# Reloading the attention heads' q, k and v inside the eighth RWKV iteration, with the cosine product on GpSimd

## What is computed

```
def _rope(x, pos):
    ...
    cos, sin = jnp.cos(ang)[:, None, :], jnp.sin(ang)[:, None, :]
    x1, x2 = x32[..., :half], x32[..., half:]
    return jnp.concatenate([x1 * cos - x2 * sin, x2 * cos + x1 * sin], axis=-1)
...
q_h = _rope(q_b.reshape(bsz, t_len, N_HEADS_B, HEAD_B), pos)
k_hb = _rope(k_b.reshape(bsz, t_len, N_HEADS_B, HEAD_B), pos)
v_hb = v_b.reshape(bsz, t_len, N_HEADS_B, HEAD_B)
```

## Time and profile before

| | |
|---|---|
| median of 3 runs | 2375.22 us (2374.91 to 2377.22) |
| the profiled execution | 2377.97 us, of which 2376.1 us is the span from the first to the last instruction |
| TensorE busy | 2279.6 us, 96% of the span |
| VectorE, ScalarE, GpSimd busy | 1151.1, 958.5 and 105.8 us |
| mean granted TensorE clock | 0.978 of full speed |
| eighth RWKV iteration | about 981 to 1058 us |
| head stage | about 1058 to 1087 us |
| cached pages, eight sequences | about 1087 to 1270 us |

### The profile page before, as it was taken

How to read it: one execution, slowest core, us unless ns; L and a number is a source line. 1 busy time by engine, 2 the same in 40 slices (tenths; PEclk the granted TensorE clock), 3 DMA queues, 4 the chain that set the end, 5 groups by cost and what they waited for, 6 DMA issues and landing times. The chain is left out here.

```text
span 2376.1 us, 49467 instructions
## 1 busy us (share of the span) xinstructions
PE 2279.6 (96%) x19735; PEld 2015.9 (85%) x19735; DVE 1151.1 (48%) x1907; ACT 958.5 (40%) x1413; POOL 105.8 (4%) x224
## 2 busy tenths in 40 slices
PE   6999899999999999978998999799999999999998
PEld 3889788887878878645666999799999999999998
DVE  4456635345353543425454655645545545544443
ACT  2433424334343443316553333454555554433333
POOL 0000001000000000100000000000100100000000
PEclk9999999999999999959998999999999999999999
DMA  9985556565666656567996555355555555555544
GB/s 347 308 286 148 160 182 182 178 192 178 191 184 187 187 171 198 185 206 245 381 388 235 165 164 160 106 163 164 168 163 164 168 163 164 168 164 164 161 151 127
DMA packets 328136, 461.20 MB, mean 194 GB/s; under 512 B 37432, under 2 KB 221282, under 8 KB 327538
## 3 DMA queue, kind: packets, MB, share of 16 engines
q1 hardware_dynamic: 319757, 450.22, 59.6%
q10 hardware_dynamic: 8215, 8.59, 1.1%
HBM read 442.86 MB, written 15.86 MB: 193 GB/s over the span
## 5 line engine op out<-in xcount | busy, mean ns | idle before, releaser
L954 ACT ACTIVATE whi<-raw 128x1024 fp32r<-128x1024 f32 (+1 forms) x512 | 527.2, 1030 | 893.1 <-PE ps L2021 861.8
L2021 PE MATMUL ps<-hhi,whi 128*128 128x288 f32 x2736 | 832.2, 304 | 10.0 <-DVE hlo L1479 6.4
L2021 PE MATMUL ps<-hhi,wlo 128*128 128x288 f32 x2736 | 808.0, 295 | 0.0
L2021 PE MATMUL ps<-hlo,whi 128*128 128x288 f32 x2736 | 807.3, 295 | 0.0
L1428 DVE TENSOR_TENSOR wlo<-raw,whi 128x1024 fp32r<-128x1024 f32 (+1 forms) x400 | 470.9, 1178 | 625.7 <-ACT whi L954 625.6
L2021 PEld LDWEIGHTS ps<-hhi,whi 128*128 128x128 f32 x2736 | 514.9, 188 | 73.0 <-issue 52.5
L2021 PEld LDWEIGHTS ps<-hlo,whi 128*128 128x128 f32 x2736 | 515.3, 188 | 1.2
L2021 PEld LDWEIGHTS ps<-hhi,wlo 128*128 128x128 f32 x2736 | 514.9, 188 | 0.0
L2021 PE MATMUL ps<-fhi,whi 128*128 128x288 f32 x704 | 208.2, 296 | 2.8 <-DVE wlo L1428 2.8
L2021 PE MATMUL ps<-fhi,wlo 128*128 128x288 f32 x704 | 207.7, 295 | 0.0
L2021 PE MATMUL ps<-flo,whi 128*128 128x288 f32 x704 | 207.3, 294 | 0.0
(11 more groups left out here) (399 smaller groups left out, 2753.6 us busy)
## 6 DMA issues: line engine op xcount, KB each, us to landing
raw<-in_w_up SPq DMA_DIRECT2D x352, 256.0 KB, 2.9
raw<-in_w_ada SPq DMA_DIRECT2D x128, 512.0 KB, 4.8
raw<-in_w_in SPq DMA_DIRECT2D x112, 512.0 KB, 4.5
raw<-in_w_down SPq DMA_DIRECT2D x88, 512.0 KB, 3.8
kpage<-in_cache_v SPq DMA_DIRECT2D x64, 512.0 KB, 5.9
raw<-in_w_in SPq DMA_DIRECT2D x72, 384.0 KB, 5.4
kpage<-in_cache_k SPq DMA_DIRECT2D x40, 512.0 KB, 5.2
ada_d<-in_w_ada SPq DMA_DIRECT2D x32, 512.0 KB, 5.9
```

The costliest lines, as they stand in the source:

```text
L954: return act.activation(o, i, ACT.Copy, **k)
L2021: return pe.matmul(out, lhsT, rhs, start=start, stop=stop, **k)
```

## The change

- The buffer `qk` gets the shape `[P, HB, 2, T]` (q and k of a head side by side) and another place: directly behind `osb`, so that its heads 0 to 3 don't overlap what the end of the eighth iteration still uses. `vq` keeps its place at the start of the region.
- v of all heads (one transfer, 1152 KB) is issued by SP within the eighth iteration, after slab 5 and the state stores there, once `mixed` and `spilled` allow it.
- q and k of heads 0 to 3 (two transfers of 576 KB) are issued when `send_turned` and `y_done` of the eighth iteration have come, ahead of the last `pair_stores`. q and k of heads 4 to 7 are issued after `ya_lo`, as before.
- TensorE's `rotate(0)` waits for `gn_roots`, the state rows and the load of heads 0 to 3. The waits for `ya_lo`, `ada_in_mod` and v come behind it.
- The product with cos moves from VectorE to GpSimd, one 128x576 operation for each head, which waits for `rotated` of that head; VectorE waits for it (`cos_done`) between its two remaining operations.
- The waits for the stores of the states move from SP to ScalarE, ahead of its first copy of k and v.

The places and the counts:

```
+        qk = nxt("qk", [P, HB, 2, T])
...
-        qk = nxt("qk", [P, 2 * HB, T])
...
-        HEADS_0 = ADA_X + 48
+        HEADS_0 = ADA_X + 32
...
+        COS_0 = KA * (LEVELS - 1)
+        HEAD0 = 64 * KA
+        EARLY_H = 4
```

SP's queue:

```
                 if s == 5:
                     pair_stores(j - 1)
+                    sp.wait_ge(mixed, KA)
+                    sp.wait_ge(spilled, 16 * RG * (KA - 1))
+                    sp.dma_start(vq[:, :, :], spill[2 * HB:3 * HB, :, :].rearrange("h p t -> p h t")).then_inc(lora_in, 16)
...
+
+            def heads_load(h0, h1, done):
+                for i in range(2):
+                    sp.dma_start(qk[:, h0:h1, i, :], spill[i * HB + h0:i * HB + h1, :, :].rearrange("h p t -> p h t")).then_inc(done, 16)
+
+            sp.wait_ge(send_turned, 2 * KA)
+            sp.wait_ge(y_done, KA)
+            heads_load(0, EARLY_H, heads_in[0])
             pair_stores(KA - 1)
-
-            def heads_load(h0, h1, done):
-                for dst, t in ((qk, 0), (qk, HB)):
-                    sp.dma_start(dst[:, t + h0:t + h1, :], spill[t + h0:t + h1, :, :].rearrange("h p t -> p h t")).then_inc(done, 16)
-                sp.dma_start(vq[:, h0:h1, :], spill[2 * HB + h0:2 * HB + h1, :, :].rearrange("h p t -> p h t")).then_inc(done, 16)
-
             sp.wait_ge(ya_lo, KA)
-            sp.wait_ge(sstate_out, 16 * NB * KA)
-            sp.wait_ge(pstate_out, 16 * KA)
-            sp.wait_ge(reloaded, ADA_X + 64)
-            heads_load(0, 1, reloaded)
-            heads_load(1, 3, heads_in[0])
-            heads_load(3, HB, heads_in[1])
-
+            heads_load(EARLY_H, HB, heads_in[1])
```

GpSimd, behind its eight iterations:

```
+            for h in range(HB):
+                pool.wait_ge(rotated, h + 1)
+                pool.tensor_tensor(qk[:, h, :, :], qk[:, h, :, :], c("cos").unsqueeze(1).to_broadcast([P, 2, T]), ALU.mult).then_inc(cos_done, 1)
```

ScalarE, ahead of its loop over the heads:

```
             act.wait_ge(reloaded, ADA_X + 64)
+            act.wait_ge(sstate_out, 16 * NB * KA)
+            act.wait_ge(pstate_out, 16 * KA)
```

VectorE, `rope`:

```
-                two = qk[:, h:2 * HB:HB, :]
+                two = qk[:, h, :, :]
                 b2 = 2 * (h % 2)
                 own.inc(TTn(rt, ps[:, b2:b2 + 2, 0:T], bc(c("sin").unsqueeze(1), [P, 2, T]), ALU.mult))
-                own(TTn(two, two, bc(c("cos").unsqueeze(1), [P, 2, T]), ALU.mult))
+                dve.wait_ge(cos_done, COS_0 + h + 1)
+                own.wait()
                 TTn(two, two, rt, ALU.add).then_inc(roped, 1)
```

TensorE, behind its eight iterations:

```
-            pe.wait_ge(ya_lo, KA)
+            pe.wait_ge(gn_roots, KA)
             pe.wait_ge(sstate_rows, 2 * KA)
             pe.wait_ge(pstate_rows, KA)
-            pe.wait_ge(ada_in_mod, ADA_G)
...
-                loaded = {0: (reloaded, ADA_X + 112), 1: (heads_in[0], HEADS_0), 3: (heads_in[1], HEADS_0)}
+                loaded = {0: (heads_in[0], HEADS_0), EARLY_H: (heads_in[1], HEADS_0)}
...
             rotate(0)
+            pe.wait_ge(lora_in, HEAD0 + 16)
+            pe.wait_ge(ya_lo, KA)
+            pe.wait_ge(ada_in_mod, ADA_G)
             for h in range(HB):
```

More of the change, by code:

```diff
@@ L526, in build @@
         tile_added = roped
+        cos_done = et_done
         stages = {}
```

12 lines of the change are left out of this document (6 added, 6 removed).

## The result

The changed kernel took 2371.51 us in the median of 11 runs (2367.45 to 2374.5), the kernel before, run beside it, 2377.28 in the median of 11 (2374.29 to 2382.4). The ratio is 0.9975 [0.9967, 0.9983]: 5.8 us less, where 7.8 had been forecast. The forecast time, 2367.4, was 4.1 us too low, and the range up to 2371.0 missed the median by 0.5 us. Part of that is not the change: the three runs of the kernel before from which I started had a median of 2375.22, and all 105 runs of it in this study have 2377.2. The profiled execution of the changed kernel took 2369.53 us, with a span of 2367.6.

What follows compares the result with a forecast made beforehand. The bound was taken to be the chain from group norm through `ya_lo`, head loads and eight heads to the first key page, with later stages following its start. 7.5 + 0.5 - 0.2 = 7.8 us less gave 2367.4 us, range 2364.5 to 2371.0.

Steps and rivals of the forecast that it cites:

- Rival D: Key pages: their transfers set the end whatever the start, so the change gives nothing, 2375 us; chance 2%.
- Part 1: Start of the head stage: early q and k loads make `rotate(0)` free and bring the first transpose 7.5 us earlier.
- just in time: State stores behind the early loads: landed by 1060.4 at the pessimistic end, ScalarE's first copy due about 1061; cost 0, at most 1 us.
- Part 2: Eighth iteration: the early v load fits an idle DMA gap and costs 0.2 us, between 0 and 3.3.
- Rival C: Eighth iteration: the v load falls into the full DMA stretch and 3.3 us go, 2370.5 us; chance 6%.
- Part 3: Head loop: the cosine on GpSimd, 1.21 us an operation, gains 0.5 us, between 0 and 1.6.
- rival B: Head loop: VectorE's two-input sums slow GpSimd's operation to 2.4 us; gain only 6.1 us, 2369.1 us; chance 6%.
- F: Head loop: GpSimd's operation becomes the cadence; slower from 3.3 us an operation, 2381 us at 4 us; chance 2%.
- A: Head stage: TensorE's lower clock stays for four more heads, 5.8 us go back, 2373.2 us; chance 7%.
- E: Head loop: ScalarE becomes the bound at 2.0 us a head, keys 9.5 to 10.1 us earlier, 2365.1 to 2365.7 us; chance 5%.
- the clock decides, not VectorE: Head loop: cadence 2.49 us with the lower clock until about 1065, 2.27 with the full clock throughout.

Runs made afterwards that it cites:

- the kernel held to `ya_lo`: Changed kernel with one wait more: GpSimd's first cosine product waits for `ya_lo`; 2370.99 us, ratio 0.9969 to the kernel before.
- loads alone: Changed kernel with the cosine product put back on VectorE, early loads kept; 2372.69 us, ratio 0.9969 to the kernel before.
- cosine alone: Kernel before with only the cosine product moved to GpSimd, loads as they were; 2375.74 us, ratio 0.9993.
- free-running ring: Changed kernel with `rotate(1)` also early and GpSimd's products written to four buffers of their own, not waiting for `rotated`; 2368.96 us, ratio 0.9971.
- side products: Early loads with the cosine on VectorE, plus three two-input GpSimd products beside the group norm; one trace, reciprocal to `yalo` 6.16 us against 4.41.

## Why the prediction was right and wrong

**What bounds the kernel: right.** The stage of the pages moved as a whole. Keys to the last values took 187.93 us before and 188.06 after, while it began 7.43 us earlier by the clock of the trace; over all sixteen traces that stage lies between 186.0 and 190.0 us, with the early loads or without. Rival D, that the transfers set the end whatever the start, is out.

**Part 1, 7.5 us: right in size, but not all of it is the loads'.** `yalo` to the first transpose fell from 10.20 to 2.76, 7.44 us (7.1 against the other trace of before, whose load came sooner). From the start of the reciprocal the forecast had the first transpose at 7.14 us (1059.83 less 1052.69); it was at 8.08, and at 7.17 in the kernel held to `ya_lo`, without the loss in the norm. The loads let `rotate(0)` begin at 1052.60, 5.8 us from their issue, 0.7 more than the 5.1 of my estimate. By the clock of the trace that was 1.4 to 2.4 us before the estimated time only because the issue came at 1046.81 and not at 1049.30. The store of the states, due "just in time", cost nothing: ScalarE's first copy, at 1062.12, waited for the transposes. But parts 1 and 3 are not two separate terms. Part 1 counted only the sine product and the sum for head 0, as if the cosine had moved already; with the cosine on VectorE "turn" falls by 6.93 and not by 7.44, and "heads" grows by 0.31 even with the clock back early (17.84 to 18.15). The sum of both parts was foreseen, 8.0, and the split of it was not: about 6.6 us for the loads, and 1.2 for GpSimd on top of them, of which the norm takes 0.9 back. The one trace of the loads alone as it stands says 5.6 for the loads, because the lower clock lasted longer in it.

**Part 2, 0.2 us: nothing that can be seen.** In three traces TensorE stood idle for the sixth pair of slabs, and it could start 39.60 us (changed) and 39.64 (loads alone), both with the early v, and 39.62 (cosine alone, where v is loaded as before) after the iteration's first matmul. The pair itself takes the 3.28 us of the earlier trace rows. TensorE's timeline of the changed kernel:

```profile
1020.60 3.28 PE L2033 MATMUL ps<-raw,scT 128*32 128x512 f32 x8 [2.83 <-DMA raw<-in_w_ada]
```

Rival C is out. v fits into the gap of the earlier trace rows. To the end states the iteration took 60.7 us in the mean of the twelve traces with the early v and 60.1 in that of the four without, but single traces lie between 57.9 and 63.3, so that says neither a cost nor none.

**Part 3, 0.5 us: the operation right, the place missed.** GpSimd's product takes 1.20 us, the line through the earlier trace rows gave 1.21. From the first transpose of head 0 to that of head 7 it is 17.00 us instead of 17.34, seven steps of 2.43, a gain of 0.34. Of the clock, the forecast held both ends open, and the granted clock was 0.91 over the heads (1060 to 1077). All eight products took 1.20 or 1.21 us, so rivals B and F are out for this kernel; A is out, since the clock was back at 2.4 GHz 2.9 us behind the first transpose, and E, since the steps were 2.43 us and not 2.0. That "the clock decides, not VectorE" was half right. The first two steps, in part at the lower clock, took 6.0 to 7.0 us together in these kernels. But once the clock was back, the last four steps took 9.20 to 9.27 us together in all six traces with the cosine on VectorE, and 8.66 or 8.67 in all seven with the cosine on GpSimd and `rotate` as in the change: 0.15 us a head, as much as the forecast took off the latency of a head (0.1 to 0.2).

**The step that failed** is the term that isn't in the sum: the norm, -0.9 us. The prediction weighed a contention of GpSimd and VectorE in the head loop alone, in one direction alone (rival B: GpSimd's operation stretched by VectorE's sums). It had itself put `rotate(0)` between the load and `yalo`, with GpSimd starting "when the head is rotated", so the first product was likely to fall into the norm or on `yalo`; what VectorE does there was not looked at. In the norm it is VectorE's instruction that is held, to three times its length, while GpSimd's is hardly longer. The Trainium skill ("GPSIMD Engine Reference", section "Key points") says that the two contend for SBUF when VectorE's instruction is in a 2-port perf mode or has two SBUF inputs. The trace agrees for the norm's `TENSOR_TENSOR` (0.46 to 1.34 us); the `TENSOR_SCALAR`, which reads one tile and a column, was held as well (0.43 to 1.34), and whether it ran in such a mode no view here shows. The kernel held to `ya_lo` shows what this term was worth: without it the stretch is 26.07 us, 7.81 less than the 33.88 of before, and the forecast was 7.8. That it agrees to 0.01 us is in part luck, as the two traces of before differ by 0.33.

The hold works in the other direction too, as rival B had it, and the trace of the kernel before could have shown it. The prediction says that no row shows a GpSimd operation stretched. Its rows don't; but behind them, in the "up" stage, 21 of 44 copies of 128x16 took 1.27 us instead of 0.20, each begun beside a split of VectorE. GpSimd's timeline there and VectorE's, both of the kernel before:

```profile
1543.34 1.27 POOL L940 COPY ext<-sconvT 128x16 f32 x1 [4.70 <-DVE cv L1985]
```

```profile
1543.33 1.23 DVE L1428 TENSOR_TENSOR wlo<-raw,whi 128x1024 fp32r<-128x1024 f32 x1 [0.17 <-ACT whi L954]
```

**The account.** Forecast 7.8 = 7.5 + 0.5 - 0.2. Measured in the stretch 6.9 = 7.44 + 0.36 - 0.91. The measured median lies 0.5 us outside the range, and at least two things put it there, each large enough by itself: the norm's 0.9, and 2.0 from the level I started from, which is no part of the mechanism. From the later median of 2377.2 for before, 7.8 us would have been 2369.4, and the 6.9 of the traces 2370.3, against 2371.5 in the first 11 runs and 2372.5 in all 32. **Open** are the last 1 to 2 us between the stretch (6.9) and the runs (5.9, 6.4, 4.5; 4.7 by the pooled medians, 5.3 by the means). It may be spread: the three intervals reach from 2.4 to 8.6 us. One row of the stage table could hold a real loss: from the iteration's last copy to the reciprocal, 5.97 and 6.10 us before, and 7.39, 6.54 and 7.12 after. What differs there is the clock. The slab pair of that stretch takes 1.06 us in the trace of before and 1.94 in that of the changed kernel:

```profile
1046.71 1.94 PE L2033 MATMUL ps<-raw,scT 128*32 128x512 f32 x8
```

Of the twelve traces of kernels with the early v, five have 7.0 us or more here and the others 5.84 to 6.54, mean 6.53; the four without it have 5.97 to 6.15, mean 6.07. That would be 0.5 us on average if it were real; with four traces on one side it isn't settled, and neither are the 0.7 us of the iteration itself (part 2).

No version beats the changed kernel in a way that the runs can tell. By the traces the free-running ring is 1.35 us better and the hold to `ya_lo`, one more wait, 0.9.

## What to carry to other kernels

When work is given to GpSimd, look up not only what its own operation costs, but what VectorE runs in the same microseconds, and the other way round, and count the first instance apart: an earlier load moved the first product out of the loop for which it had been weighed and into a serial chain. Make its first start wait for the end of that chain (here one wait, 0.9 us by the trace). When an experiment is read from one trace, look at the granted clock of that trace before its difference is given to the edit: of the 1.37 us that the heads seemed to lose in the kernel with the loads alone, 1.06 were absent from two other traces of the same head stage. And take a starting level from more than three runs: their median was 2.0 us below that of all 105. The stretch between two fixed events repeated to 0.04 and 0.33 us in the traces, where whole runs had a standard deviation of 2.8.

## What the runs showed of the hardware

VectorE and GpSimd took turns at SBUF, and the one that had begun first went on at its own pace. A `TENSOR_TENSOR` or `TENSOR_SCALAR` of VectorE with all its tiles in SBUF that begins while an elementwise operation of GpSimd runs is held until that is about to end, and then takes its own time: 0.43 us became 1.34 and 1.39, 0.46 became 1.34, 1.25 and 1.09, 0.76 became 1.66. The short ones ended 0.16 to 0.32 us behind GpSimd's end, the sum of 0.76 us 0.61 behind it (1056.72 against 1056.11), each by its own length less 0.14 to 0.27. So an overlap costs VectorE what is left of GpSimd's operation, 0.9 us at most for one of 1.2.

In the same way GpSimd was held when VectorE had begun first. Its product of 1.20 us took 1.37 in the second trace of the changed kernel and 1.73 and 1.72 in the ring, and ended 1.06 or 1.07 us behind the end of VectorE's instruction each time, its own length less 0.14; its copy of 128x16 took 1.27 us instead of 0.20 beside VectorE's split of 1.23.

Not held were the reciprocal (1.95 us beside the side products, of which the two that lay beside it took 1.40 and 1.41 us), a memset that began beside a product (0.27 us, in the kernel held to `ya_lo`), and the sine product, which reads PSUM. VectorE's timeline in the changed kernel and GpSimd's, for head 2:

```profile
1063.86 0.76 DVE L1784 TENSOR_TENSOR rtmp<-ps,cst 128x576 f32<-128x576 f32 x1 [1.34 <-PE ps L2033]
```

```profile
1063.84 1.20 POOL L942 TENSOR_TENSOR qk<-qk,cst 128x576 f32<-128x576 f32 x1 [2.11 <-PE ps L2033]
```

A GpSimd copy of 128x576, with one input, takes 0.66 to 0.77 us and holds VectorE in the same way for less time (0.46 to 0.84).
